# Regrouping the expert passes of a decoder layer into units of 32 rows, with two named experts loaded early

## The reference, cut to what matters

```
g_sel   = argmax(h @ rg_w + rg_b)                      # one of 4 groups
top_v, top_i = top_k(expert logits of that group, 2)   # two of its 8 experts
gate    = p_group * softmax(top_v)
y[token] += gate * ((silu(h @ w_gate[e]) * (h @ w_up[e])) @ w_down[e])
```

## Time and profile before

| what | us |
|---|---|
| median of 3 runs | 1450.31 (1446.19 to 1454.56) |
| the profiled execution | 1454.74 |
| its span, first to last instruction | 1452.9 |
| expert stage, first row transpose to the end of the span | 842 to 1452.9 |

### The profile page before, as it was taken

One profiled execution on the slowest core, in us unless ns is written; L12 is line 12 of the kernel. 1 busy time (PEld: TensorE's weight loads), 2 busy tenths in 40 slices (PEclk: granted clock), 3 DMA queues, 4 the chain that ended last, 5 costly groups with the idle time before them and its releaser, 6 DMA issues.

```text
span 1452.9 us, 15254 instructions
## 1 busy us (share of the span) xinstructions
PE 1336.4 (92%) x5616; PEld 691.3 (48%) x5616; DVE 506.4 (35%) x1193; ACT 251.5 (17%) x487; POOL 175.2 (12%) x170
## 2 busy tenths in 40 slices
PE   6999999999999888879998679999999999999985
PEld 3444554644446566654555534443444444444432
DVE  2079683133546565651344512111111111111100
ACT  5000114132124333331111010000000000000000
POOL 1000005222000000000000011211212112112111
PEclk9999999899999899999999589999999999999998
DMA  6011010100120110302221098959999999999970
GB/s 256 0 60 58 1 58 0 58 6 6 48 66 5 36 35 5 121 1 93 101 87 73 28 395 338 400 195 350 424 404 406 412 407 391 402 397 389 403 272 18
DMA packets 51272, 261.70 MB, mean 180 GB/s; under 512 B 21571, under 2 KB 21843, under 8 KB 38908
## 3 DMA queue, kind: packets, MB, share of 16 engines
q1 hardware_dynamic: 42684, 243.72, 41.9%
q0 software_dynamic: 8320, 16.81, 4.7%
q10 hardware_dynamic: 192, 0.17, 0.1%
HBM read 247.52 MB, written 23.64 MB: 187 GB/s over the span
## 4 chain that ended last, share of the span: by engine, by line
PE 69%; issue 8%; DMA 7%; DVE 7%; POOL 3%; DVEq 3%; ACT 1%; SPq 0%; POOLq 0%; ACTq 0%
PE ps L1176 18%; PE ps L1178 13%; PE ps L895 9%; PE ps L1081 8%; PE ps L899 4%; DMA arena<-in_ex_up 3%; PE ps L1026 3%; DMA arena<-in_ex_down 2%; PE ps L1057 2%; POOL arena L2020 2%; PE ps L1042 2%; PE ps L1162 1%; PE ps L1102 1%; DMA arena<-in_ex_gate 1%; DVE arena L1495 1%
## 5 line engine op out<-in xcount | busy, mean ns | idle before, releaser
L1176 PE MATMUL ps<-arena 128*128 128x512 f32 x768 | 336.7, 595 | 1.9 <-ACT arena L1971 0.8
L1176 PEld LDWEIGHTS ps<-arena 128*128 128x128 f32 x768 | 144.3, 191 | 171.9 <-issue 169.3
L1178 PE MATMUL ps<-arena 128*64 128x512 f32 x480 | 213.5, 601 | 8.3 <-DMA arena<-in_ex_up 4.5
L1179 PE MATMUL ps<-arena 128*64 128x512 f32 x480 | 213.6, 601 | 0.0
L899 PE MATMUL ps<-arena 128*128 128x512 f32 x384 | 173.6, 605 | 0.0
L895 PE MATMUL ps<-arena 128*128 128x512 f32 x320 | 137.6, 592 | 0.0
L1740 DVE TENSOR_TENSOR arena<-arena,ps 128x512 f32<-128x512 f32 x26 | 17.9, 689 | 328.8 <-PE ps L1176 202.3
L1178 PEld LDWEIGHTS ps<-arena 128*64 128x64 f32 x480 | 64.7, 138 | 138.1 <-issue 136.2
L1081 PE MATMUL ps<-arena 128*128 128x512 f32 x256 | 112.1, 597 | 0.8 <-DVE arena L1532 0.8
L899 PEld LDWEIGHTS ps<-arena 128*128 128x128 f32 x384 | 72.6, 195 | 83.0 <-issue 81.5
L2076 POOL DMA_INDIRECT out<-arena x26 | 42.0, 1615 | 473.2 <-DVE arena L1746 473.2
(11 more groups left out here) (299 smaller groups left out, 1297.7 us busy)
## 6 DMA issues: line engine op xcount, KB each, us to landing
arena<-in_ex_gate SPq DMA_DIRECT2D x32, 2048.0 KB, 21.7
arena<-in_ex_up SPq DMA_DIRECT2D x32, 2048.0 KB, 24.2
arena<-in_ex_down SPq DMA_DIRECT2D x32, 2048.0 KB, 24.0
arena<-in_w_in SPq DMA_DIRECT2D x5, 2048.0 KB, 7.8
arena<-in_x SPq DMA_DIRECT2D x16, 512.0 KB, 6.2
arena<-bias_by_distance SPq DMA_DIRECT2D x4, 1024.0 KB, 5.9
arena<-in_w_out SPq DMA_DIRECT2D x8, 512.0 KB, 7.3
out<-arena SPq DMA_DIRECT2D x8, 512.0 KB, 2.6
```

Of the source, the lines that this page charges most:

```text
L1176: last = mm(ps[:, to, :], rowsT[:, k, :], weights[left][:, k, cols], **f)
L1178: mm(ps[0:HALF, to, :], rowsT[:, k, 0:HALF], weights[left][:, k, cols], **f)
L1179: last = mm(ps[HALF:P, to, :], rowsT[:, k, HALF:P], weights[right][:, k, cols], **f)
```

## The change

Ranks are now made over all experts but 0 and 1, which are named (`FIXED`) and take the last two ranks. The cover goes in units of 32 rows: 224 rows for rank 0, 192 for rank 1, 160 for ranks 2 and 3, 128 for ranks 4 to 7, 96 for ranks 8 to 13, 64 for ranks 14 to 24, 32 for ranks 25 to 29, and 128 for each named expert. There are 23 passes in the order of the string: F a named expert alone, W up to 128 rows of one of the first eight, T 96 rows of one expert and 32 of another, P 64 and 64, R what is over from the expert of the last W, with another. That makes 10 "whole", 7 "three" (two products for the left expert, with 64 and 32 stationary columns, and one of 32 for the right) and 6 "halves".

The weights of the named experts don't wait for the ranks: four of the six parts are issued between the tiles of the output projection, the other two after it. A pass with two experts adds its result to `out` in two indirect DMAs, one for each expert's rows, the second after the first has landed. (Both experts may hold the same token.) The extra slots are 20 instead of 18, worked out two to a pass.

```
+FIXED = (0, 1)
+N_FIXED = len(FIXED)
+def expert_passes():
+    ranks = {"whole": iter(range(8)), "three": iter(range(8, 14)), "two": iter(range(14, 27 - N_FIXED)),
+             "one": iter(range(27 - N_FIXED, EXPERTS - N_FIXED)), "fixed": iter(range(EXPERTS - N_FIXED, EXPERTS))}
+    passes, whole = [], None
+    for kind in "FFPTWRPTWRPWRTWRWTWPWWP":
+        if kind == "F":
+            passes.append(("whole", (next(ranks["fixed"]), 0), None))
+        elif kind == "W":
+            whole = next(ranks["whole"])
+            passes.append(("whole", (whole, 0), None))
+        elif kind == "T":
+            passes.append(("three", (next(ranks["three"]), 0), (next(ranks["one"]), 0)))
+        elif kind == "P":
+            passes.append(("halves", (next(ranks["two"]), 0), (next(ranks["two"]), 0)))
+        elif whole == 0:
+            passes.append(("three", (0, 1), (next(ranks["one"]), 0)))
+        elif whole == 1:
+            passes.append(("halves", (1, 1), (next(ranks["two"]), 0)))
+        else:
+            passes.append(("three", (next(ranks["three"]), 0), (whole, 1)))
+    return passes
-EXTRA = 18
+EXTRA = 20
+BLOCKS = {"whole": ((0, 128, 0),), "halves": ((0, 64, 0), (64, 128, 1)),
+          "three": ((0, 64, 0), (64, 96, 0), (96, 128, 1))}
...
 @block.sync
+            beside_output = [("gate", 0), ("up", 0), ("down", 0), ("down", 1)]
             for t in range(TILES):
+                if t < len(beside_output):
+                    part, n = beside_output[t]
+                    load_weights(part, n, FIXED[n], weights_in[part][n])
                 sp.wait_ge(x2_done, t + 1)
                 sp.dma_start(out[t * P:(t + 1) * P, :], xs[:, t % 2, :]).then_inc(x2_out[t % 2], 16)
...
             sp.wait_ge(out_mm, TILES)
+            for part in ("gate", "up"):
+                load_weights(part, 1, FIXED[1], weights_in[part][1])
             sp.wait_ge(experts_known, 1)
             for _, n, _, part, s, freed in WEIGHT_ISSUES:
+                if n < N_FIXED:
+                    continue
                 if freed is not None:
                     sp.wait_ge(used[part], freed + 1)
-                if (n, part) == (0, "up"):
+                if (n, part) == (2, "gate"):
                     sp.wait_ge(rows_in[0], 16)
...
 @block.tensor
-            def times_weights(to, rowsT, n_k, weights, left, right, cols):
+            def times_weights(to, rowsT, n_k, weights, blocks, cols):
                 for k in range(n_k):
-                    f = dict(start=(k == 0), stop=(k == n_k - 1))
-                    if left == right:
-                        last = mm(ps[:, to, :], rowsT[:, k, :], weights[left][:, k, cols], **f)
-                    else:
-                        mm(ps[0:HALF, to, :], rowsT[:, k, 0:HALF], weights[left][:, k, cols], **f)
-                        last = mm(ps[HALF:P, to, :], rowsT[:, k, HALF:P], weights[right][:, k, cols], **f)
+                    for r0, r1, buf in blocks:
+                        last = mm(ps[r0:r1, to, :], rowsT[:, k, r0:r1], weights[buf][:, k, cols],
+                                  start=(k == 0), stop=(k == n_k - 1))
                 return last
...
 @block.vector
-                elif 2 <= n < 2 + EXTRA:
-                    extra_slot(n - 2)
+                elif 2 <= n < 2 + EXTRA // 2:
+                    extra_slot(2 * (n - 2))
+                    extra_slot(2 * (n - 2) + 1)
...
 @block.gpsimd
+            def add_pass(n, side):
+                u = n % 2
+                rows = rows_of(n)
+                if len(sides_of(n)) == 2:
+                    pool.wait_ge(sides_ready, 1)
+                    rows = side_rows[:, side, COLUMN[n] - N_WHOLE:COLUMN[n] - N_WHOLE + 1]
+                pool.wait_ge(y_v, n + 1)
+                if side:
+                    pool.wait_ge(y_out[u], landed_from(u, n) - 16)
+                else:
+                    at_least(pool, y_out[1 - u], landed_from(1 - u, n - 1))
+                nc.gpsimd.indirect_dma_start(out, bass.IndirectOffsetOnAxis(ap=rows, axis=0), ys[:, u, :], None,
+                                             bounds_check=SEQ - 1, oob_is_err=False, compute_op=ALU.add).then_inc(y_out[u], 16)
...
                 if n + 2 < NP:
                     gather(n + 2, n % 2, rows_of(n + 2))
                 if n:
-                    add_pass(n - 1)
+                    add_pass(n - 1, 0)
                     pool.wait_ge(row_gate_in, 16 * n)
                 fetch_gates(row_gate[:, n:n + 1], dst_of[:, COLUMN[n]:COLUMN[n] + 1])
+                if n and len(sides_of(n - 1)) == 2:
+                    add_pass(n - 1, 1)
```

More of the change, by code:

```diff
@@ L68 @@
+PASSES = expert_passes()
 NP = len(PASSES)
-EXTRA = 18
+EXTRA = 20
 SLOTS = NP + EXTRA
[L71 to L80, removed]
-def weight_loads():
[L85 to L89, removed]
+BLOCKS = {"whole": ((0, 128, 0),), "halves": ((0, 64, 0), (64, 128, 1)),
+          "three": ((0, 64, 0), (64, 96, 0), (96, 128, 1))}
@@ new lines, with experts_of @@
+OF_KIND = {kind: [n for n in range(NP) if PASSES[n][0] == kind] for kind in BLOCKS}
+BY_KIND = OF_KIND["whole"] + OF_KIND["three"] + OF_KIND["halves"]
+COLUMN = [BY_KIND.index(n) for n in range(NP)]
+N_WHOLE, N_THREE = len(OF_KIND["whole"]), len(OF_KIND["three"])
+RANKED = EXPERTS + 2 * NP - N_WHOLE
+def experts_of(n):
+    return [side[0] for side in PASSES[n][1:] if side]
+def weight_loads():
+    order = list(dict.fromkeys(s for n in range(NP) for s in experts_of(n)))
+    last = [max(n for n in range(NP) if s in experts_of(n)) for s in order]
@@ L140, in order_constants @@
     part, e = np.arange(P)[:, None], np.arange(EXPERTS)[None, :]
[L141 to L147, removed]
+    mine, block = part % EXPERTS, part // EXPERTS
+    sides = ([(s, 0) for s in range(EXPERTS)] + [PASSES[n][1] for n in BY_KIND] + [PASSES[n][2] for n in BY_KIND[N_WHOLE:]])
+    rank = np.array([s for s, _ in sides])[None, :]
+    of_block = np.array([b for _, b in sides])[None, :]
+    key = EXPERTS - 1.0 - e
+    for n, expert in enumerate(FIXED):
+        key = key - 1e6 * (n + 1) * (e == expert)
+    cols = [np.broadcast_to(key, (P, EXPERTS)), (e == mine), np.where(block == of_block, rank, -1)]
     return np.ascontiguousarray(np.concatenate([np.asarray(c, np.float32) for c in cols], 1))
@@ L609, in weights_landed, with passes_in, buffer_of_extra, sides_of @@
             return 16 * (LOADED_AS[s] // 3 + 1)
+        def passes_in(u):
+            return (NP + 1 - u) // 2
+        def buffer_of_extra(u):
+            return (NP + u) % 2
+        def sides_of(n):
+            return {"whole": ((0, 128),), "three": ((0, 96), (96, 128)), "halves": ((0, 64), (64, 128))}[PASSES[n][0]]
+        def landed_from(u, last):
+            return 16 * sum(len(sides_of(n)) for n in range(last + 1) if n % 2 == u)
         def extras_loop(eng, body, before_them=None):
@@ L762, in _, with load_weights @@
             sp.wait_ge(d_pe, len(PE_ORDER))
+            places = {"gate": w_gate, "up": w_up, "down": w_down}
+            used = {"gate": gate_mm, "up": up_mm, "down": down_mm}
+            def load_weights(part, buf, expert, landed):
+                return sp.dma_start(places[part][buf], a[f"ex_{part}"][bass.ds(expert, 1), :, :]
+                                    .rearrange("e (p k) n -> p (e k) n", p=P)).then_inc(landed, 16)
+            beside_output = [("gate", 0), ("up", 0), ("down", 0), ("down", 1)]
             for t in range(TILES):
+                if t < len(beside_output):
+                    part, n = beside_output[t]
+                    load_weights(part, n, FIXED[n], weights_in[part][n])
                 sp.wait_ge(x2_done, t + 1)
@@ L1199, in down @@
                 at_least(pe, y_v, n)
[L1200 removed]
+                blocks = landed_for("down", n)
                 for half in range(2):
[L1202 removed]
+                    last = times_weights(5 + half, actT, FC, w_down, blocks, slice(half * 512, (half + 1) * 512))
                 last.then_inc(down_mm, 1)
@@ L1217, in extra @@
             def extra(slot, u, pair):
-                turn_rows(slot, u, 16 * (pair + NP // 2 + 1))
+                b = buffer_of_extra(u)
+                turn_rows(slot, b, 16 * (pair + passes_in(b) + 1))
                 pe.wait_ge(rowsT_a, slot + 1)
@@ L1665, in _ @@
             v.wait_ge(order_mm, 2)
-            ts(slots[:, 0:16], ps[:, 5, 0:16], -1.0, None, ALU.add)
-            for side in range(2):
-                rows = slice(side * HALF, (side + 1) * HALF)
-                pairs = ps[rows, 5, 40:40 + RANKED].rearrange("p (s two) -> p s two", two=2)[:, 8:18, side]
-                ts(slots[rows, 16:NP], pairs, -1.0, None, ALU.add)
+            ts(slots[:, 0:NP], ps[:, 5, 0:NP], -1.0, None, ALU.add)
             nc.vector.drain()
@@ L2069, in fetch_gates, with add_rows @@
                                              bounds_check=2 * SEQ - 1, oob_is_err=False).then_inc(row_gate_in, 16)
-            def add_rows(slot, u, before, rows):
```

(1 more changed line is left out.)

131 lines of the change are left out of this document (75 added, 56 removed).

## The result

The changed kernel takes 1574.99 us (median of 4 runs, 1570.7 to 1576.09) against 1448.49 us for the kernel before in the same session: a ratio of 1.0861, 95% interval 1.082 to 1.0902. The forecast was 1420 us. The stated range, 1400 to 1580 us, holds the measured time only because it was stretched to the near edge of rival B; the way the time moved was forecast wrong. Rival B of the prediction, products of unlike width that don't run together, had 1579 us for its lower end, and its signs are those that follow: three passes of about 50 us, and a DMA share under 0.9.

What follows compares the result with a forecast made beforehand. Two limits 2% apart in the expert stage: TensorE's passes (577 us) and DMA weight loads (564 us). -66.5 + 32.3 + 3.4 = -30.8 us takes 1452.9 to 1422, or 1420 against the median; range 1400 to 1580 us.

Steps and rivals of the forecast that it cites:

- rival B: Three passes: columns of unlike width don't run together, 49 to 58 us each instead of 20.6; total 1579 to 1637; chance 0.21.
- I take the low end: Expert stage, three pass: its three products share the 0.43 us step as pairs do, 20.6 us a pass.
- The high end of the same sentence: Three pass: 64-column product, then the two small ones, plus width switches: 2.06 to 2.40 us per step, 49 to 58 a pass.
- the nearest row: Trace of the kernel before: a disjoint pair of 64-column products, wholly parallel, taken as the price of a three pass.
- 26 passes to 23: Expert stage: three passes less at 22.2 us each, -66.5 us of TensorE time; extra-slot loop stays empty.
- The two named experts: Six weight parts leave the expert stage for the output projection and after: DMA work 528 us instead of 564, no cost there.
- More experts per pass: Expert stage, three buffers: waits for weights 43.1 us against 10.8, +32.3 us, and +3.4 us for the lower clock.
- The ledger: Expert stage: TensorE and DMA clocks run against each other, 5.87 us a weight part; gave 1453.8 us for the kernel before.
- The two that were named: Expected signs: waits for in_ex_down near 943 and 1050 us, of about 10 us.
- Two adds per shared pass: 13 of 23 passes write out in two indirect adds; gathers stay in time, price nothing up to a landing of 14 us.
- The rest at nothing: Small work ahead of slots_ready under 0.5 us; VectorE's longer rows_left and extra-slot operations covered by its idle time: nothing.

Runs made afterwards that it cites:

- four of 32: Changed kernel with the three pass's 64-column product split into two of 32, so all four have one width (the run with one width): 1424.53 us, 0.9823 of the kernel before.
- a pair: Changed kernel with each three pass computed as two 64-column products, output partly not the reference's: 1424.95 us, 0.982 of the kernel before.
- without the early loads: Against four of 32: the six weight parts of the named experts issued after experts_known, not beside the output projection; 1444.99 us, 0.9963 of the kernel before.
- the other order: Against four of 32: passes in the order FFPPWRTWRTWRPWRPWTWPWTW, ending on a one-expert pass; 1421.58 us, 0.9805 of the kernel before.

## Why the prediction was wrong, step by step

*The step that failed* is "I take the low end": a three pass at the price of a pair, because disjoint products were wholly parallel in the rows and each switch with a price was between widths that share columns. The one disjoint pair in the trace had one width. A three pass costs 47.6 us of products instead of 20.9, 187 us over seven passes, of which some 147 are left in the time because the waits for weights and their slow products shrink. With this one term changed (four of 32, or a pair), the time is 1424.5 us where 1420 were forecast. The high end of the same sentence, 49 to 58 us, was right but for some 2 us, since a change of width costs 0.13 to 0.14 us here and not up to 0.20; what was wrong was the choice between the ends, and the chances (0.62 against 0.21).

The row that could have told was there: in the earlier trace rows a change from 64 to 128 columns cost 0.20 us and one from 128 to 64 cost 0.14. I read these as a price of shared columns. They are better read as a sign that something about the width belongs to the whole engine. The Trainium skill (TensorEngine Tiling, Key Properties, with the list under Available Configurations) says that a change of the tiling mode drains TensorE, and has 128x64 and 128x32 as two modes. The prediction gave that rule as rival B's and set it below the nearest row. The runs agree with the rule: 0.13 to 0.14 us for each change, no overlap across it, in two products or three. That a drain is what keeps them apart is the page's word; the runs show the times.

*26 passes to 23*: right. The chain has 23 passes, and no extra slot ran.

*The two named experts*: right in kind, 20.5 us instead of 27. Loads beside the output projection cost nothing there: from its first product to the first row transposes it is 181.7 us before and 181.3 after, and 179.5 and 181.3 in the runs with four of 32 with and without the early loads. In the changed kernel itself, with the DMA at a share of 0.74, they probably bring little; no run took them out there.

*More experts per pass*: right once TensorE is fast. The ledger gave 43.1 us of waits, the run with one width has 36.2. The two that were named, near 943 and 1050 us and about 10 us each, end at 946.9 (8.1 us) and 1056.3 (9.9 us). The lower clock behind five waits cost 9.8 us where the ledger had 8.5. But its rule for this, 1.7 us behind any wait of more than 2.5 us, doesn't hold run by run: the changed kernel's waits of 2.8 and 3.6 us cost nothing more (7.09 us for the products after each), and with the other order waits of 2.0 and 2.3 us cost 1.7 each.

*Two adds per shared pass*: right where it counted, wrong at the end. No gather was late, and adds landed in 11.5 us (13.9 at most), in the run with one width in 12.2 (14.1 at most). But the last pass has two experts, and its second add, 6.5 us in the chain, stands alone at the end. The ledger's fixed 15.4 us behind the last product left it out: it is 18.4 us in the changed kernel and 18.8 with one width. That is 3 and not 6.5 us more, since the last adds land faster (4.5 to 4.8 us for 6.0) and the stretch behind them is some 2 us shorter.

*The rest at nothing*: nothing showed.

*The ledger* gave a difference of -31 us, and the run with one width has -26.6. That this is so near is partly luck: by it the stage would be 580 us (1422 less 842) and it is 584.8, with 6.9 us of waits too many, 1.3 and 3.4 us too few for the slow products and the end, and some 7 us that it has nowhere. For an edit of 10 us (the order) it is too coarse, since 5.6 instead of 5.87 us a part already shifts it by 13, and the add that was to be saved at the end was not.

## What to carry to other kernels

Before a price is taken from the nearest row, ask in what that row differs: here it was disjoint like the new case, but of one width, and only the width mattered. If products are packed into column groups of TensorE, try all neighbours at the width of the narrowest one: here, in float32 with 512 moving columns, four narrow products cost what a wide one does, and a mix of 64 and 32 columns 2.3 times as much. Leave a full-width pass whole, since each change to the width of the transposes beside it costs 0.13 to 0.21 us. Before an edit at the end of a kernel, follow the queue back: an operation that must wait for the one ahead of it isn't saved by moving that one a place forward. When two resources are within a few per cent of each other, an edit that takes work from the one gains only what the other allows: 66 us less TensorE work brought 6 us alone, and 26 with 36 us of DMA work moved away.

## What the runs showed of the hardware that was not expected

- Products of 64 and of 32 columns in disjoint column groups don't overlap at all: 1.98 us a k step, against 0.86 for four of 32 or two of 64. Each change between these widths adds 0.13 to 0.14 us.
- Four products of 32 columns with four loads run in the 0.43 us of one full-width record. The Trainium skill (TensorE: Matmul & The Clock Gate, Part 3, measured speedup) has 2.38 times for three small products; in this long stream four go in the time of one.
- An indirect add under load lands in about 12 us, whether it holds a whole pass or a part of one: the median is 12.5 us before, with up to 128 rows to an add, and 12.2 in the run with one width, where 26 of the 36 adds have a part of a pass. With the queues nearly empty, at the end, it takes 4.5 to 4.8 us for each of the two adds of a pair, and 6.0 to 6.1 for three others (the last one before, and with the other order one with up to 96 rows and one with up to 128), so there the number of rows seems to count. How many rows each of them really moved isn't in the trace.
